# A hybrid trunk step on one core: z kept in half chunks, loads and the scan's steps in another order

## The reference

```
u = rmsnorm(x, g_mix)
dn_qkv, dn_z, dn_alpha, dn_beta, sb_q, sb_k, sb_v = split(u @ w_in)
qa, ka, va = split(silu(causal_conv(dn_qkv, conv_w, conv_state)))       # 4 taps per channel
g, beta = -exp(a_log) * softplus(dn_alpha + dt_bias), sigmoid(dn_beta)
o_a = gated_delta_rule(l2norm(qa) / 8, l2norm(ka), va, g, beta, s0)     # below
o_a = rmsnorm(o_a, g_out_dn) * silu(dn_z)
o_b = stick_breaking(rmsnorm(sb_q), rmsnorm(sb_k), sb_v)                # with the cached keys and values
h = x + concat(o_a, o_b) @ w_out
h = h + square(relu(rmsnorm(h, g_mlp) @ w_up)) @ w_down
h = h + sigmoid(rmsnorm(h, g_ple) @ w_ple_gate) * (p @ w_ple_proj)
```

```
a_mat = where(strict, (kb @ k^T) * decay, 0)
u, w  = solve(a_mat + I, [v * beta, kb * exp(gcum)])
v_new = u - w @ s
o     = (q * exp(g)) @ s + (q @ k^T * decay) @ v_new
s     = s * exp(g_last) + (k * exp(g_last - g))^T @ v_new
```

## Time and profile before

| | |
|---|---|
| median of 3 runs | 1837.28 us (1836.14 to 1840.3) |
| profiled execution | 1842.09 us, span 1840.4 us |
| mean granted clock of TensorE | 0.964 |
| PE busy | 1688.1 us (92%) |
| DVE busy | 718.6 us (39%) |
| POOL busy | 571.3 us (31%) |
| ACT busy | 461.8 us (25%) |
| chain that ended last | PE 78%, DVE 9%, DMA 4%, issue 3%, ACT 3%, SP's queue 3% |

### The profile page before, as it was taken

One profiled execution on the slowest core, in us unless ns is written; L12 is line 12 of the kernel. 1 busy time (PEld: TensorE's weight loads), 2 busy tenths in 40 slices (PEclk: granted clock), 3 DMA queues, 4 the chain that ended last, 5 costly groups with the idle time before them and its releaser, 6 DMA issues.

```text
span 1840.4 us, 33120 instructions
## 1 busy us (share of the span) xinstructions
PE 1688.1 (92%) x14640; PEld 1595.8 (87%) x14640; DVE 718.6 (39%) x892; ACT 461.8 (25%) x906; POOL 571.3 (31%) x284
## 2 busy tenths in 40 slices
PE   5899999995899668778999999999999999999998
PEld 5799989993566456678999999999999999999898
DVE  5653033553676567762152222121212222226322
ACT  4322113222666434432132010101010101013111
POOL 2332322311100122234244343434343434342520
PEclk9999999996999779988999999999999999999999
DMA  5212311113102445432211111111111111112121
GB/s 162 64 47 70 102 62 58 70 59 127 53 2 60 130 105 109 103 82 53 85 53 46 47 46 46 46 47 46 46 46 47 46 46 47 46 46 70 46 58 49
DMA packets 203716, 118.58 MB, mean 64 GB/s; under 512 B 74481, under 2 KB 196797, under 8 KB 203580
## 3 DMA queue, kind: packets, MB, share of 16 engines
q1 hardware_dynamic: 194080, 103.54, 20.1%
q10 hardware_dynamic: 9500, 13.02, 1.9%
HBM read 94.69 MB, written 21.84 MB: 63 GB/s over the span
## 4 chain that ended last, share of the span: by engine, by line
PE 78%; DVE 9%; DMA 4%; issue 3%; ACT 3%; SPq 3%; POOL 0%; ACTq 0%; DVEq 0%; POOLq 0%
PE psum L2168 44%; PE psum L1969 8%; PE psum L2460 5%; PE psum L1922 3%; PE psum L1923 3%; PE psum L1924 3%; PE psum L2001 2%; PE psum L2013 2%; DVE area L1694 2%; PE psum L2031 2%; DMA area<-x_scratch 1%; DMA area<-out_dram 1%; PE psum L2479 1%; DVE area L1521 1%; DVE act_lo L1836 1%
## 5 line engine op out<-in xcount | busy, mean ns | idle before, releaser
L2168 PE MATMUL psum<-act_hi,w_round 128*128 128x352 f32 x1920 | 367.9, 324 | 0.7 <-ACT area L1351 0.4
L973 POOL TENSOR_TENSOR w_round<-w_plain,ones 128x1024 fp32r<-128x1024 f32 x80 | 175.8, 2198 | 511.7 <-DMA w_plain<-in_w_up_dram 229.3
L2168 PEld LDWEIGHTS psum<-act_hi,w_round 128*128 128x128 f32 x1920 | 319.9, 189 | 1.8 <-issue 1.0
L2168 PE MATMUL psum<-hid_hi,w_round 128*128 128x352 f32 x1344 | 257.5, 323 | 0.4 <-DVE hid_lo L1866 0.4
L2168 PEld LDWEIGHTS psum<-hid_hi,w_round 128*128 128x128 f32 x1344 | 222.3, 188 | 0.7 <-DVE hid_lo L1866 0.7
L1843 DVE TENSOR_TENSOR area<-psum,area 128x1056 f32<-128x1056 f32 x72 | 90.5, 1257 | 308.1 <-PE psum L2168 308.1
L2168 PE MATMUL psum<-act_lo,w_round 128*128 128x352 f32 x960 | 207.0, 324 | 0.0
L974 POOL TENSOR_TENSOR w_round<-w_plain,w_round 128x1024 fp32r<-128x1024 f32 x80 | 198.8, 2485 | 6.3
L1450 ACT ACTIVATE hid_hi<-area 128x1056 fp32r<-128x1056 f32 x28 | 30.4, 1087 | 589.1 <-DVE area L1859 589.1
L1922 PE MATMUL psum<-w_round,act_hi 128*128 128x256 f32 (+1 forms) x576 | 167.0, 290 | 3.9 <-ACTq L1108 3.2
L1923 PE MATMUL psum<-w_round,act_hi 128*128 128x256 f32 (+1 forms) x576 | 164.0, 285 | 0.0
(11 more groups left out here) (293 smaller groups left out, 2433.2 us busy)
## 6 DMA issues: line engine op xcount, KB each, us to landing
w_plain<-in_w_up_dram SPq DMA_DIRECT2D x32, 512.0 KB, 4.0
w_plain<-in_w_down_dram SPq DMA_DIRECT2D x32, 512.0 KB, 3.4
w_plain<-in_w_in_dram SPq DMA_DIRECT2D x14, 1024.0 KB, 5.3
conv_scratch<-area ACTq DMA_DIRECT2D x12, 512.0 KB, 2.7
area<-in_x_prompt_dram SPq DMA_DIRECT2D x8, 512.0 KB, 3.7
w_plain<-in_cache_k_dram SPq DMA_DIRECT2D x4, 1024.0 KB, 5.5
w_plain<-in_w_out_dram SPq DMA_DIRECT2D x8, 512.0 KB, 5.0
w_plain<-in_x_prompt_dram SPq DMA_DIRECT2D x8, 512.0 KB, 5.0
```

What stands on the lines that cost most here:

```text
L973: own.link(pool.tensor_tensor(hi, ring_raw(n), ones[:, 0:1].to_broadcast([P, RB]), ALU.mult))
L2168: last = pe.matmul(bank(bank_set(tile) + c)[:, 0:CH], w(k), a(k)[:, CH * c:CH * (c + 1)], start=(begins and k == ks[0] and w is w_h and a ...
```

## The change

Five parts are edited.
1. *Start.* The load of `gmix_b` counts on a semaphore that nothing else uses at that time (`ab_loaded`), and DVE waits for this one alone; the other nine vectors are waited for later. The transpose of the parameters on PE moves behind the second tile, their copy on ACT too. SP loads the second weight block behind the fourth tile of x instead of behind the ninth.
2. *z.* `z_scratch` is laid out by half chunks: (half chunk, head parity, token, 4 heads x 64). A full tile of z is written with two DMAs, and the scan's `z_in` reads a chunk with one DMA instead of four.
3. *SP between the token blocks and the attention.* The two early loads of shifted V stand ahead of the loads of cached keys, and the stores of the tails and the second load of cached keys behind the last load of V.
4. *Masks.* `first_masks` has two instructions instead of four, over all partitions, with a mask of two columns; `first_transposed` has one add instead of four.
5. *The scan.* The order of the functions in the loops of SP, POOL, ACT, DVE and PE is another. On DVE the levels 4 and 8 follow each other with two short instructions between them, and stand behind `key_matrix`; the steps (i + 1, 0) and (i + 1, 1) stand in the same round. On SP the dump of the next chunk stands ahead of the scatter. On PE all four `heads_part` stand in one round. The orders of ACT and POOL, cut below, are changed to match.

```diff
-    z_dram = nc.dram_tensor("z_scratch", (T, W), F32).ap()
+    z_dram = nc.dram_tensor("z_scratch", (2 * NTT, 2, HD, W // 2), F32).ap()
...
-        odd16 = sb("odd16", [P, 1])
+        odd16 = sb("odd16", [P, 2])
...
-        def below16(x, r):
-            at = 32 * (r % 2)
-            return x[32 * r:32 * r + 32, :, at:at + 16]
+        def left16(x):
+            return x.rearrange("p m (a c) -> p m a c", a=2)[:, :, :, 0:16]
...
+        def z_count(n):
+            return 16 * sum(1 if tile_rows[j % NTT] < P else 2 for j in range(n % 2, n, 2)) if n < HALF else \
+                16 * (2 * NTT - 1)
...
-            sp.dma_start(gmix_b, g_mix.broadcast_to([P, D])).then_inc(vecs_loaded, 16)
+            sp.dma_start(gmix_b, g_mix.broadcast_to([P, D])).then_inc(ab_loaded, 16)
...
+                if t == 3:
+                    sp.wait_ge(raw_free, 2)
+                    sp.dma_start(w_raw[:, 1, :].rearrange("p (k n) -> p k n", k=KT),
+                                 win[:, :, SBCOL + 256:SBCOL + 512]).then_inc(raw_loaded[1], 16)
...
-            block_in(1, 1, win[:, :, SBCOL + 256:SBCOL + 512])
...
-            sp.wait_ge(tails_c, 1)
-            for n, dst in enumerate((conv_prompt, conv_sample)):
-                sp.dma_start(dst[0, 0].rearrange("i (m b) -> (i m) b", b=P),
-                             tails_out[36 * n:36 * n + 36, :]).then_inc(tails_stored, 16)
...
-                n = min(real(q), HD)
-                for g in range(subs(q)):
-                    first = P * chunk(q) + HD * g
-                    z = z_dram[first:first + n, :].rearrange("i (k u e) -> u i k e", u=2, e=HD)
+                c = 2 * chunk(q)
+                if q:
+                    sp.dma_start(d_z[:].rearrange("p (g k) e -> p g (k e)", g=2),
+                                 z_dram[c:c + 2].rearrange("g u i x -> (u i) g x")).then_inc(z_loaded, 16)
+                else:
                     for u in range(2):
-                        sp.dma_start(d_z[HD * u:HD * u + n, WT * g:WT * (g + 1)], z[u]).then_inc(z_loaded, 16)
+                        sp.dma_start(d_z[HD * u:HD * u + TS, 0:WT].rearrange("p k e -> p (k e)"),
+                                     z_dram[c, u, 0:TS, :]).then_inc(z_loaded, 16)
...
-            sp.wait_ge(raw_free, 14 + 2)
-            for n in range(2):
-                cache_keys_in(n)
+            for u in range(2):
+                sp.wait_ge(z_stored[u], z_count(HALF))
             sp.wait_ge(v_stored, 32)
-            sp.wait_ge(z_silu, HALF)
-            for u in range(2):
-                sp.wait_ge(z_stored[u], 16 * NTT)
             sp.dma_start(v_early[1:P, 0, :], v_out[0:P - 1, :]).then_inc(vs_loaded[0], 16)
             sp.dma_start(v_early[:, 1:4, :], v_out[P - 1:4 * P - 1, :].rearrange("(t p) c -> p t c", p=P))\
               .then_inc(vs_loaded[0], 16)
+            sp.wait_ge(raw_free, 14 + 2)
+            cache_keys_in(0)
             sp.wait_ge(dense_ready, NC)
             sp.dma_start(v_diff[:, 4:NT, :], v_out[4 * P - 1:TP - 1, :].rearrange("(t p) c -> p t c", p=P))\
               .then_inc(vs_loaded[1], 16)
+            sp.wait_ge(tails_c, 1)
+            for n, dst in enumerate((conv_prompt, conv_sample)):
+                sp.dma_start(dst[0, 0].rearrange("i (m b) -> (i m) b", b=P),
+                             tails_out[36 * n:36 * n + 36, :]).then_inc(tails_stored, 16)
+
+            cache_keys_in(1)
...
             def at_out(q):
                 sp.wait_ge(at_made, q + 1)
+                if q:
+                    sp.wait_ge(gathered, 16 * q)
...
             for i in range(-3, CHUNKS + 1):
-                if i >= -1 and at(i + 2):
-                    sums_in(i + 2)
-                if at(i):
-                    t_in(i)
+                if i == 1:
+                    sp.wait_ge(consts_made, 6)
+                if at(i - 1):
+                    z_in(i - 1)
+                if i >= 0 and at(i + 2):
+                    conv_v_in(i + 2)
+                if i >= -2 and at(i + 3):
+                    conv_qk_in(i + 3)
+                if at(i + 2):
+                    at_out(i + 2)
                 if at(i + 1):
-                    lanes_in(i + 1)
-                if at(i):
-                    x_in_blocks(i)
-                if i == CHUNKS - 1:
+                    lanes_out(i + 1)
+                if i >= -2 and at(i + 3):
+                    sums_in(i + 3)
+                if at(i + 2):
+                    lanes_in(i + 2)
+                if at(i + 1):
+                    t_in(i + 1)
+                if at(i + 1):
+                    x_in_blocks(i + 1)
+                if i == CHUNKS - 2:
                     for done in (kg_made, qg_made, qry_ready, kv_turned, cn_made):
                         sp.wait_ge(done, CHUNKS)
                     for n in range(DN_RING, RING):
                         ring_in(n)
-                if at(i - 1):
-                    if i == 1:
-                        sp.wait_ge(consts_made, 6)
-                    z_in(i - 1)
...
-                if i >= -2 and at(i + 3):
-                    conv_qk_in(i + 3)
-                if at(i + 1):
-                    lanes_out(i + 1)
-                if at(i + 2):
-                    at_out(i + 2)
-                if i >= -1 and at(i + 3):
-                    conv_v_in(i + 3)
...
+                for g in range(1 if rows < P else 2):
+                    of_chunk = slice(HD * g, min(HD * (g + 1), rows))
+                    act.dma_start(z_dram[2 * t + g, :, 0:of_chunk.stop - of_chunk.start, c // 2:(c + HC) // 2]
+                                  .rearrange("u i x -> i u x"),
+                                  z_buf[of_chunk, n % 2, :].rearrange("i (u x) -> i u x", u=2))\
+                       .then_inc(z_stored[n % 2], 16)
...
-                for r in range(4):
-                    last = act.activation(below16(d_m[:, 0:m], r), below16(mat(0, 0, m), r), ACT.Copy,
-                                          scale=odd16[32 * r:32 * r + 32, :])
+                for r in range(2):
+                    last = act.activation(d_m[:, 0:m, 32 * r:32 * r + 16], mat(0, 0, m)[:, :, 32 * r:32 * r + 16],
+                                          ACT.Copy, scale=odd16[:, r:r + 1])
...
-            dve.wait_ge(vecs_loaded, 160)
+            dve.wait_ge(ab_loaded, 16)
...
-                for r in range(4):
-                    t = below16(d_t[:, q % 2, 0:m], r)
-                    last = tt(t, below16(mat(0, 0, m), r), t, ALU.add)
-                last.then_inc(t16_made, 1)
+                t = left16(d_t[:, q % 2, 0:m])
+                tt(t, left16(mat(0, 0, m)), t, ALU.add).then_inc(t16_made, 1)
...
             for i in range(-4, CHUNKS):
-                if i > 0:
-                    new_state(i, 1)
                 if at(i):
                     output_sums(i)
                 if at(i + 1):
                     rest_of_values(i + 1, 0)
+                if at(i):
+                    normed_output(i)
+                if at(i):
+                    gated_output(i)
+                if at(i + 1):
+                    new_values(i + 1, 0)
                 if at(i + 3):
                     query_matrix(i + 3)
-                if at(i):
-                    normed_output(i)
-                if at(i + 1):
-                    new_values(i + 1, 0)
                 if at(i + 4):
                     decay_differences(i + 4)
-                if at(i):
-                    gated_output(i)
-                if at(i + 3):
-                    lanes_begin(i + 3)
                 if at(i + 1):
                     new_state(i + 1, 0)
-                if at(i + 3):
-                    lanes_middle(i + 3)
                 if at(i + 4):
                     unit_norms(i + 4)
                 if at(i + 3):
-                    lanes_end(i + 3)
-                if at(i + 1) and i >= 0:
-                    rest_of_values(i + 1, 1)
+                    lanes_begin(i + 3)
                 if at(i + 4):
                     key_matrix(i + 4)
+                if at(i + 3):
+                    lanes_middle(i + 3)
+                if at(i + 1) and i + 1 > 0:
+                    rest_of_values(i + 1, 1)
                 if at(i + 2):
                     first_transposed(i + 2)
-                if at(i + 1) and i >= 0:
+                if at(i + 3):
+                    lanes_end(i + 3)
+                if at(i + 1) and i + 1 > 0:
                     new_values(i + 1, 1)
                 if at(i + 3):
                     decayed_queries(i + 3)
+                if at(i + 3):
                     decayed_keys(i + 3)
                 if at(i):
                     rest_of_output(i)
+                if at(i + 1) and i + 1 > 0:
+                    new_state(i + 1, 1)
...
+            pe.wait_ge(vecs_loaded, 144)
+            pe.transpose(bank(3)[:, 0:100], param_rows[0:100, :], ident[0:100, 0:100]).then_inc(par_t, 1)
...
-            for i in range(-4, CHUNKS + 1):
```

(52 more changed lines are left out.)

90 lines of the change are left out of this document (46 added, 44 removed).

## The result

The changed kernel takes 1811.73 us (median of 4 runs, 1809.28 to 1817.45), the kernel before 1836.71 beside it: ratio 0.9864, 95% interval 0.9838 to 0.9891. The profiled execution took 1817.45 us (span 1815.7) against 1842.09 (span 1840.4), 24.6 us less; the forecast of it was 1820.6. Both profiled executions are long ones of their kernel, 5.7 us above the median after and 5.4 before.

A forecast was written before the change was run, and what follows sets the result against it. It saw room in the attention's opening hole, the scan (closed by a loop through DMA) and the first 62 us. Terms -15 - 7 + 1.5 - 1 = -21.5 took 1842.09 to 1820.6; less 4.8 to the median, 1816, range 1799 to 1832.

The forecast's parts named there:

- the scan: DeltaNet scan: shorter rounds -7.4 us, slower fill +4.6, slower drain +1.5; together about -1 us, bounds -13 and +14.
- the V load: Start of the prompt attention: shifted V arrives early, DVE's whole 15.57 us wait goes; -15 us, bounds -11 and -18.
- the start: First 62 us: DVE waits for one load, and the second weight block's split moves earlier; -7 us, bounds -3 and -9.
- z: z's token blocks: two stores per full block with 512-byte runs cost +1.5 us, bounds 0 and +4.
- its split falls into the first tiles, which gives back half a microsecond: At the start: POOL's split of the second weight block, loaded earlier, lands among the first tiles and costs 0.5 us.
- eight rounds: the first 20.1, then seven of 21.1: Scan rounds, the first on half-size chunk 0: 167.8 us in all, against 175.2 before.
- The fill and the drain: Scan's ends: first levels' end 4.6 us later; four output projection pieces in one round cost 1.5 us at the end.
- 0.6 us slower behind the load: Scan's round: the chain after X's load was to be 0.6 us slower, the part ahead of it 2.3 faster.
- its 20.3: Scan's round from one levels' end to the next, through X's load, without the clock's cost: 20.3 us.
- rounds open with 3 to 4 us of half clock: Scan on PE: after a gap, half clock slows outputs and state change by 1.8 us, making the round 21.1 us.
- the long half clock: Rival, 17%: in the scan, half clock lasts through the square sums, 1.8 us more in seven rounds; 1829 us.
- the half clock through whole rounds: Rival, 7%: in the scan PE never regains full clock within a round, 8 us longer in seven rounds; 1872 us.

The follow-up runs named there:

- the two other profiles of this order: Kernel before with only the masks and the scan's new orders, ratio 0.9947; and the changed kernel with z stored and loaded as before, 1807.66 us.
- Taking PE's wait away: Changed kernel with DVE's second new values between the two products of level 8 and the second new state earlier: ratio 0.9878.
- taking the key matrix from behind X: Changed kernel with TensorE's key products ahead of the first matrices: 1801.33 us, ratio 0.9808; the same swap with z as before: 1800.17 us.
- the gap filled: Changed kernel with each second matrix product made four times instead of once, the same result written again: ratio 0.9893.

## Why the prediction held, and where its steps did not

The median of 1811.73 us lies 4.3 below the forecast of 1816, and that closeness is in part luck: in the profiles the scan gained 7.4 us more than forecast, the V load, the start and z together 4.2 less.

**The V load** (-15; measured -13.6 in the change, -15.1 alone). Right in mechanism and size: the wait named in the earlier trace rows was what the part took away, and nothing of like length took its place. In the change DVE now waits 6.8 us for ACT's silu with its table loads, a wait that was 4.1 us before.

**The start** (-7; measured -5.1). The split's departure was worth 4.8 us alone, the dropped wait 2.3 where I had 1, and the two together less than their sum. The profile counts here too: in the eight kernels with the change's start z's first silu came at 210.05 to 211.86, which is 5.1 to 6.9 us ahead of the kernel before. The step that failed is "its split falls into the first tiles, which gives back half a microsecond": it stretched two scalings by 2.9 and 3.0 us. How much of that is on the path is not shown. That the early start would be worth little stood on the right row; it left out that the first scaling itself stood behind a split.

**z** (+1.5; measured +2.4). Inside its bounds of 0 and +4. The price came mostly from the runs of 512 bytes, not from the second issue; the prediction had named both.

**The scan** (-1; measured -8.4). Inside the bounds of -13 and +14, but this is the step that was mis-sized, and within it the term "eight rounds: the first 20.1, then seven of 21.1", 167.8 us against 162.3 (161.1 and 157.1 in the two other profiles of this order, where the whole scan gained 10.5 and 14.3 us). The five middle rounds were 107.7 against 105.5, and 103.3 and 101.9 in the others, on both sides of the forecast. The other three were 17.4, 19.0 and 18.2 where the sum had 20.1, 21.1 and 21.1, 7.7 us less (4.6 and 7.0 in the others). They hold less: the first two have one step of the state to do or none, and the last has no square sums, key products and key matrix. The sum gave two of them the length of a full round and the first 1.0 less. That this is why they are short is argued, not shown: in the order before, the second and the last round have a step or the square sums less as well, and took 22.5 and 22.7 us, where the five in the middle averaged 22.1. The fill and the drain were 0.9 and 0.7 us better than their terms. In the round's own sum, "0.6 us slower behind the load" should be 0.4 (10.5 us against 10.1); its 20.3 is right by its terms.

**The loop.** The prediction named one loop, levels' end, scatter, load of X, first matrices, key products, key matrix, levels, and a wait on PE that costs clock. Both are there, and in the changed kernel they are of nearly the same length: in some rounds X is late (TensorE's matmuls waited up to 3.1 us for it), in others the new values are (the round of 23.0 us has no wait for X). Taking PE's wait away left X (rounds as long); taking the key matrix from behind X took 6.6 to 11 us off the eight rounds. Of "rounds open with 3 to 4 us of half clock" the trace shows more in the longest round (behind a wait of 2.87 us, 0.50 from 728 to 737) and about that in the next (behind a wait of 3.22 us, 0.50 from 751.4 to 753.4 and 1.00 from 755); what it costs could not be told apart from the X loop at this length. The Trainium skill, TensorE: Matmul & The Clock Gate, section "HAM oscillation", says that bursts of matmuls with a DMA wait between them pay the slow start once per burst. The trace agrees as far as the clock goes, here with waits for DVE: with the gap filled, four of the last five rounds opened at 2.4 GHz (1.00), and the fifth fell to 0.50 from 727 to 729. That this would shorten the round did not follow.

**The rivals.** Rounds under 19.5, which the prediction named as a sign of being wrong, were three of eight, all at the edges; the long half clock came in some of the rounds (square sums of 3.58 to 3.78 us in four of the seven that have them), without reaching its 1829; the wait in place of V's and the half clock through whole rounds did not come.

## What to carry to other kernels

Rounds at the edge of a pipelined loop can hold less work; price them by what they hold and by what closes them, not by the full round. When two loops of like length close a round, removing one can show nothing, so ask of each order which instruction needs nothing of the late one and move that ahead: one swap on TensorE's list took 6.6 to 11 us off the rounds. A long GpSimd instruction beside VectorE costs by who starts first: here a start a third of a microsecond earlier went with a scaling four shorter. And compare an order's gain over several profiles: one order's rounds took 157 to 162 us.

## What the runs showed of the hardware

A scaling of DVE that starts 0.17 us behind a POOL split of 4.50 us takes 5.42 instead of 1.28; one that starts 0.16 us ahead of it takes 1.28, and the split 5.50. With 0.03 us ahead by the trace it took 5.62, and the split 4.50. Stores of a tile of z landed in 2.1 us (median) with runs of 512 bytes and in 1.7 with 1 KB, and the runs, not the number of stores, set most of the 2.4 us in z's blocks.
